# A hybrid decoder layer on one core: another hand-over to attention, and swish made by one ScalarE activation

## The chip, the cores and the metric

The kernel runs on one core of a Trainium2 chip. The metric is the device time of one execution in microseconds; the median of three runs is 1112.57 (1110.75 to 1113.08). TensorE (PE) multiplies, ScalarE (ACT) and VectorE (DVE) work element by element, GpSimd (POOL) too; SP only issues transfers, and ACT and POOL issue some as well. Every engine runs its own list of instructions in order and waits on semaphores for the others.

## What is computed

One decoder layer over 1024 positions of width 1024, all in fp32. Cut to what matters here:

```python
h = rmsnorm(x, ln_pre);  z = h @ w_in
c_val, c_glu, c_gate, q, k, v, a_gate, g_conv, g_attn = split_columns(z)
u  = c_val * sigmoid(c_glu)
c  = silu(layernorm(causal_depthwise_conv31(u) + b_dw, ln_g, ln_b))
ya = ((c @ w_pw) * silu(c_gate)) @ w_br_conv
yb = (sliding_window_sink_attention(rope16(q), rope16(k), v) * silu(a_gate)) @ w_br_attn
x  = x + rmsnorm((sigmoid(g_conv) * ya + sigmoid(g_attn) * yb) @ w_out, ln_post)
x  = x + sigmoid(x @ w_ple_gate) * (p @ w_ple_proj)
```

There are 16 query heads and 2 key heads of 64 values; of each head the first 16 values are rotated by position (rope), the other 48 are not. The window is 128, the block 128.

## The kernel before, in words

Everything lies transposed: 128 partitions hold channels, the 1024 positions run along the free dimension, and a matrix of 1024 channels is 8 rows of 128 x 1024. Every product is made from a high and a low part of its operands: ScalarE rounds a tile to fp32r (`high`, `split_high`, `..._high`), another engine subtracts to get the rest (`tile_low`, `low`, `..._low`), and TensorE adds three products. Nothing is scheduled by a compiler: the order on each engine is written out by hand, and a semaphore names each dependence.

The program's stages on TensorE are: the per-layer embedding product; a few plain tiles of `h @ w_in`; 18 pairs of output rows by a scheme of seven products (`EARLY`, L953), the last of them k and v; two plain tiles Q0 and Q0+1, which are query rows 3 and 7 (L766); attention (`attention(p)`, p from 0 to 15; block n = p // 2 and key head p % 2), in which each p also multiplies one half of a tile of the convolution's gate, C0 + n (L1101); 8 tiles D0 of the attention's gate; 8 tiles E0 for the attention branch; the seven products again, stage F for `c @ w_pw` and stage G for `@ w_br_conv` (`seventh`, L1193), in 4 pairs each; and the two last matrices.

**The turn from the pairs to attention.** Query rows 0, 1, 2, 4, 5 and 6 have been stored to memory (`GATES` rows 3 KT + j) during the pairs; k and v come last, in `ring` (`k_raw`, `v_t`). VectorE rotates several heads in one instruction, so the 16 rotated values of each head are collected: `pack0` holds 16 rows for each of the two key heads and 6 query half rows, `pack1` 6 query half rows. SP issues all of it in this order (L668 to L692): the angle tables `cos_t` and `sin_t`, three rows' `pack` (16-row transfers, two per query row), the two k groups from `k_raw`, the other six `pack`, four `kdup` transfers (the 48 plain values of each key head, to two places), the six whole query rows to `qo`, the weights C0, and then, after the rotation, `unpack(0)` (six 16-row transfers back to `qo`), four to `kdup`, `unpack(1)`, and the weights C0 + 1. `unpack` waits for a finished rotation (`rope_done`) and for all query rows (`q_loaded`, 96).

VectorE (L2192 to L2194) runs `rope(0)` on pack0, `rope(1)` on pack1 and `rope_in_place(0)` on query row 3, four or five full-width steps each, the last two one behind the other through `rope_done` and `last_roped`. The first scores (`scores(0, 0)`, L981) wait for `conv_done`, `k_dup`, `unpacked[0]` and `last_roped`.

**In attention**, for each p ScalarE first reads the gate product of p - 1 (`gate_half`, L1574: a tanh to `tanh_t`, a copy to `gate_val`), splits the next gate weights (`next_high`), copies outputs and turned probabilities, and makes eight exponentials (`exps`, L1549). VectorE finds maxima, makes the gate as (tanh + 1) * value in `ring` (its own `gate_half`, L2254), and normalises. At p = 0 ScalarE's list has `high(C0 // 2, 1)`, the split of the weights C0 + 1, ahead of the first `exps`. The gate is stored to memory and read back in stage F.

**Stage F.** Per pair i, ScalarE copies four products aside (`keep`, L1686), reloads the two gate rows by `load_gates` (L1699), and makes high parts of weights (`block_high`). VectorE's `take` (L2409) combines quarters and multiplies each with its gate half, in `ring`; `block_low` (L2387) makes the low part of the weights that TensorE uses some products later, in the same list. The sums of the results for stage G (`y_sum`, `part_high`, `part_low`) come at the end of pair 3.

The layer norm's swish is a tanh on ScalarE (`norm_tanh`, L1651) and two VectorE steps (`norm_finish`, L2360); the attention's gate a tanh and one VectorE step. The factor 1/2 of x/2 * (1 + tanh(x/2)) is applied later, in the splits.

Of the kernel before, what the change touches and what calls it, by code (L numbers as in the profile page):

```python
# [25 lines left out]
P = 128  # L26
# [9 lines left out]
HD = 64  # L36
# [72 lines left out]
def build(nc, dram):  # L109
    with ExitStack() as ctx:  # L110
# [29 lines left out]
        cos_t = at("cos_t", [S], F32, RE + 12 * KB)  # L140
# [6 lines left out]
        gate_val = at("gate_val", [HALF], F32, RE + 22 * KB)  # L147
# [11 lines left out]
        v_last = at("v_last", [P], F32, GB + 28 * KB - 192)  # L159
# [46 lines left out]
        for name, n in (("half_g", KT), ("half_b", KT), ("two_b", KT), ("mean_sq", 8), ("rstd", 8), ("expo", 8), ("sq_sums", 8), ("sinks", 16),  # L206
                        ("smax", 16), ("nmax", 16), ("esink", 16), ("denom", 16), ("rden", 16)):
            names[name] = at(name, [n], F32, small)
            small += 4 * n
        half_g, half_b, two_b, mean_sq, rstd, expo, sq_sums = (names[n] for n in (  # L210
            "half_g", "half_b", "two_b", "mean_sq", "rstd", "expo", "sq_sums"))
# [31 lines left out]
        tanh_ready = sem("tanh_ready")  # L243
# [30 lines left out]
        gated = sem("gated")  # L274
# [24 lines left out]
        ln_tanh = sem("ln_tanh")  # L299
# [109 lines left out]

        def pack_of(j):  # L410

            return (0, j + 1) if j < 3 else (1, j - 4)
# [175 lines left out]
        def _(sp):  # L588
# [51 lines left out]
            def pack(j):  # L640

                n, c = pack_of(j)
                for par in range(2):
                    sp.dma_start(packs[n][32 * c + 16 * par:32 * c + 16 * par + ROT, :],
                                 GATES[par * HD:par * HD + ROT, 3 * KT + j, :]).then_inc(packed[n], 16)

            def unpack(n):

                sp.wait_ge(rope_done, n + 1)
                sp.wait_ge(q_loaded, 96)  # L650
                for j in range(4 * n, 4 * n + 3):
                    c = pack_of(j)[1]
                    for par in range(2):
                        sp.dma_start(qo[par * HD:par * HD + ROT, j, :],
                                     packs[n][32 * c + 16 * par:32 * c + 16 * par + ROT, :]).then_inc(unpacked[n], 16)
# [4 lines left out]
            sp.dma_start(w_second[:], WALL[:, Q0 + 1 + PLE_STEPS, :]).then_inc(w_loaded[1], 16)  # L660
            sp.wait_ge(spilled[0], 16 * len(SPILLS))
            sp.wait_ge(spilled[1], 16 * len(SPILLS))
            sp.wait_ge(pos_loaded, TRIG_STORED)
            sp.wait_ge(early_made, EARLY_PRODUCTS - 1)
            def rows_of_angles(first, last):
                return TRIG[first:last].rearrange("n (f c) a -> (n f) (c a)", f=8).rearrange("(a r) s -> a r s", a=1)

            for table, first, last in ((cos_t, 0, 1), (sin_t, 1, 3)):  # L668
                count = 8 * (last - first)
                sp.dma_start(table[:], rows_of_angles(first, last).to_broadcast([P // count, count, S])).then_inc(pos_loaded, 16)  # L670
            for j in (0, 1, 2):
                pack(j)
# [3 lines left out]
            for j in (4, 5, 6):  # L676
                pack(j)
            for g in range(2):
                for half in range(2):
                    sp.dma_start(kdup[half * HD + ROT:(half + 1) * HD, g, :],  # L680
                                 k_raw[g * HD + ROT:(g + 1) * HD, :]).then_inc(k_dup, 16)
            for j in (0, 1, 2, 4, 5, 6):
                sp.dma_start(qo[:, j, :], GATES[:, 3 * KT + j, :]).then_inc(q_loaded, 16)
# [4 lines left out]
            for g in range(2):  # L688
                for half in range(2):
                    sp.dma_start(kdup[half * HD:half * HD + ROT, g, :], packs[0][ROT * g:ROT * g + ROT, :]).then_inc(k_dup, 16)  # L690
            unpack(1)
            load_tile(C0 + 1)  # L692
# [62 lines left out]
        def _(pe):  # L755
# [225 lines left out]
            def scores(p, jp):  # L981
# [365 lines left out]
        def _(act):  # L1347
# [175 lines left out]

            act.wait_ge(v_turned, 1)
# [5 lines left out]
            nc.scalar.activation(v_last[lower_half], turned_values[lower_half, NB - 1, :], ACT.Copy).then_inc(v_ready, 1)  # L1530
            query_tile(0)
# [42 lines left out]
            def gate_half(p):  # L1574
# [7 lines left out]
                if p > 1:  # L1582
                    act.wait_ge(gated, p - 1)
                nc.scalar.activation(tanh_t[:, half], gate_bank(p), ACT.Tanh, scale=0.5).then_inc(tanh_ready, 1)
                if p > 0:
                    act.wait_ge(gated, p)
                nc.scalar.activation(gate_val[:], gate_bank(p), ACT.Copy).then_inc((half_free, ps_free[n % 2])[h], 1)

            def spill_gate(n):

                act.wait_ge(gated, 2 * n + 2)
                spill(GATES[:, n + KT, :], n % 2)
# [41 lines left out]
            for m in range(KT):  # L1634
# [6 lines left out]
                split_high(o_hi, m, qo[:, m, :], 0.5)  # L1641
# [9 lines left out]
            def norm_tanh(k):  # L1651

                act.wait_ge(ln_scaled, k + 1)
                if k >= 2:
                    act.wait_ge(ln_full, k - 1)
                nc.scalar.activation((tanh_t, work)[k % 2][:], conv[:, k, :], ACT.Tanh, bias=half_b[:, k:k + 1],
                                     scale=half_g[:, k:k + 1]).then_inc(ln_tanh, 1)

            def c_high(k):
# [5 lines left out]
                nc.scalar.activation(dst, src, ACT.Copy, scale=0.5).then_inc(hi_ready, 1)  # L1665
# [11 lines left out]
            def sum_high(n):  # L1677
# [6 lines left out]
                nc.scalar.activation(s_hi[:, n], sum_of(n), ACT.Copy, scale=0.5).then_inc(s_hi_ready, 1)  # L1684
# [24 lines left out]

            def part_high(name, k):  # L1710
# [9 lines left out]
                nc.scalar.activation(part_split(name, rows)[0], part_raw(name, rows), ACT.Copy, scale=0.5).then_inc(part_hi, 1)  # L1720
# [10 lines left out]
            for m in range(KT):  # L1731
# [6 lines left out]
                for k in norm_beside(m):  # L1738
                    norm_tanh(k)
# [132 lines left out]
        def _(dve):  # L1872
# [131 lines left out]
            own.step(nc.vector.tensor_scalar(half_g[:], cols[:, COL["ln_g"]:COL["ln_g"] + KT], 0.5, None, ALU.mult))  # L2004
            own.step(nc.vector.tensor_scalar(two_b[:], cols[:, COL["b_dw"]:COL["b_dw"] + KT], 2.0, None, ALU.mult))
            own.step(nc.vector.tensor_scalar(half_b[:], cols[:, COL["ln_b"]:COL["ln_b"] + KT], 0.5, None, ALU.mult))
# [185 lines left out]
            rope(0, P, slice(0, S), 128)  # L2192
            rope(1, 96, slice(0, S), 96)
# [60 lines left out]
            def gate_half(p):  # L2254

                n, h = divmod(p, 2)
                half = slice(h * HALF, (h + 1) * HALF)
                dve.wait_ge(tanh_ready, p + 1)
                dve.wait_ge(spilled[n % 2], (n // 2) * 16 + 16 * len(SPILLS))
                if h == 0:  # L2260
# [466 lines left out]
```

## Time and profile before

| | |
|---|---|
| median of three runs | 1112.57 us |
| the profiled execution: its time, its span | 1111.12 us, 1109.3 us |
| granted TensorE clock, mean | 0.995 |
| busy: PE, PEld, DVE, ACT, POOL | 1090.7, 887.9, 884.9, 485.2, 316.2 us |
| DMA | 155.19 MB, mean 140 GB/s |
| chain that ended last: PE | 91% of the span |

The span runs from the first to the last instruction; the execution's time has 1.8 us around it. Times of the views are microseconds from the span's start. "PE busy" counts matmuls in flight. A wait of an engine is idle time, put down to what ended it. A transfer's time to landing runs from its issue until its semaphore has the full count of 16. The granted clock is 1.00 at 2.4 GHz and 0.50 at 1.2 GHz.

### The profile page before, as it was taken

Reading aid. Unit: us, or ns where it says so; the run is one execution under the profiler, and the core shown is the slowest. Engines: PE = TensorE matmul, PEld = TensorE weight load, DVE = VectorE, ACT = ScalarE, POOL = GpSimd, SP = SyncE. Lnnn points to the kernel's source line nnn. Section 1 sums busy time; section 2 is a strip of 40 time slices with the busy share of each in tenths; the row PEclk is TensorE's granted clock in tenths of the full one; section 3 lists DMA queues with packets and bytes.
Section 4 is the critical chain, followed back from the end, with each engine's and each line's share of the span. In section 5 each row is a group of like instructions: output and inputs, shape, how many; then the busy total and the mean of one; then the engine's idle time right before and its main releaser. Section 6 shows DMA issues by size and latency. Waiting matters only on the chain.

```text
span 1109.3 us, 16255 instructions
## 1 busy us (share of the span) xinstructions
PE 1090.7 (98%) x5992; PEld 887.9 (80%) x5992; DVE 884.9 (80%) x1243; ACT 485.2 (44%) x927; POOL 316.2 (29%) x252
## 2 busy tenths in 40 slices
PE   9999999999999998799999999999999999999998
PEld 7888888888888886577777888888888888888887
DVE  5998989999999975598985788777768878466875
ACT  6633343443334432466674442433435426344332
POOL 1068888887888851200000000000000000000000
PEclk9999999999999999899999999999999999999999
DMA  9802231322232329777742111464544843344655
GB/s 343 350 1 78 78 113 42 114 77 77 94 134 77 114 80 236 206 208 198 187 131 77 39 57 38 133 217 143 180 134 129 319 137 127 95 128 138 192 188 189
DMA packets 52976, 155.19 MB, mean 140 GB/s; under 512 B 6281, under 2 KB 7049, under 8 KB 50857
## 3 DMA queue, kind: packets, MB, share of 16 engines
q1 hardware_dynamic: 38216, 96.58, 27.1%
q10 hardware_dynamic: 12384, 40.90, 10.5%
q0 software_dynamic: 2304, 16.78, 6.4%
q8 instruction: 43, 0.70, 0.2%
q14 instruction: 29, 0.23, 0.1%
HBM read 123.86 MB, written 45.19 MB: 152 GB/s over the span
## 4 chain that ended last, share of the span: by engine, by line
PE 91%; DMA 3%; SPq 2%; DVE 2%; ACT 1%; issue 1%; DVEq 0%; ACTq 0%
PE psg L766 31%; PE psg L953 31%; PE psb L1193 11%; PE psg L1101 7%; PE psg L790 2%; PE psg L1072 1%; PE psb L1015 1%; PE psg L1193 1%; DMA qo<-gates 1%; PE psg L873 1%; PE psg L819 1%; PE psg L1146 1%; PE psg L1033 1%; ACT probs L1558 1%; PE psg L1067 1%; DMA p_raw<-pT 1%
## 5 line engine op out<-in xcount | busy, mean ns | idle before, releaser
L1251 POOL TENSOR_TENSOR pair_w<-early_raw,pair_w 128x512 fp32r<-128x512 f32 x117 | 155.5, 1338 | 83.1 <-ACT pair_w L1443 83.1
L953 PE MATMUL psg<-early_hi,pair_w 128*128 128x512 f32 x576 | 177.3, 389 | 0.0
L2095 DVE SCALAR_TENSOR_TENSOR psb<-conv,cols,psb 128x510 f32<-128x510 f32 (+6 forms) x196 | 137.7, 745 | 0.0
L953 PE MATMUL psg<-h_hi,pair_w 128*128 128x512 f32 x432 | 133.0, 389 | 0.0
L953 PEld LDWEIGHTS psg<-early_hi,pair_w 128*128 128x128 f32 x576 | 108.1, 188 | 22.4
L1443 ACT ACTIVATE pair_w<-early_raw 128x512 fp32r<-128x512 f32 x117 | 71.4, 627 | 112.3 <-POOL early_raw L1267 81.1
L1234 POOL TENSOR_TENSOR rstd<-mean_sq,expo 128x4 f32<-128x4 f32 x3 | 3.1, 1020 | 382.9 <-DVE mean_sq L1896 363.4
L953 PE MATMUL psg<-early_lo,pair_w 128*128 128x512 f32 x288 | 112.0, 389 | 0.0
L1882 DVE TENSOR_TENSOR w_lo<-w_raw,w_hi 128x1024 fp32r<-128x1024 f32 x57 | 69.8, 1224 | 41.2 <-ACT w_hi L1356 37.5
L953 PEld LDWEIGHTS psg<-h_hi,pair_w 128*128 128x128 f32 x432 | 81.1, 188 | 16.8
L1356 ACT ACTIVATE w_hi<-w_raw 128x1024 fp32r<-128x1024 f32 x58 | 61.2, 1056 | 65.0 <-PE psg L766 34.6
L2095 DVE SCALAR_TENSOR_TENSOR psb<-fir_sum,fir_taps,psb 128x511 f32<-128x511 f32 (+14 forms) x120 | 89.4, 745 | 0.0
L953 PE MATMUL psg<-h_lo,pair_w 128*128 128x512 f32 x216 | 84.0, 389 | 0.0
L1267 POOL TENSOR_TENSOR early_raw<-early_raw 128x512 f32<-128x512 f32 x54 | 75.0, 1390 | 4.2
L1193 PE MATMUL psb<-s_hi,pair_w 128*128 128x512 f32 x240 | 73.9, 389 | 0.0
L953 PEld LDWEIGHTS psg<-early_lo,pair_w 128*128 128x128 f32 x288 | 54.1, 188 | 11.3
L766 PE MATMUL psg<-h_hi,w_hi 128*128 128x512 f32 x192 | 59.6, 392 | 0.0
L766 PE MATMUL psg<-h_hi,w_lo 128*128 128x512 f32 x192 | 59.2, 389 | 0.0
L766 PE MATMUL psg<-h_lo,w_hi 128*128 128x512 f32 x192 | 59.1, 389 | 0.0
L1675 ACT ACTIVATE pair_w<-block_raw 128x512 fp32r<-128x512 f32 x56 | 34.5, 626 | 41.7 <-PE psb L1193 21.5
L1193 PEld LDWEIGHTS psb<-s_hi,pair_w 128*128 128x128 f32 x240 | 45.0, 188 | 9.4
L1101 PE MATMUL psg<-h_hi,w_hi 128*128 128x512 f32 x128 | 52.1, 407 | 0.0
(348 smaller groups left out, 2511.8 us busy)
## 6 DMA issues: line engine op xcount, KB each, us to landing
w_raw<-weights SPq DMA_DIRECT2D x60, 512.0 KB, 3.6
gates<-ring ACTq DMA_DIRECT2D x30, 512.0 KB, 3.6
w_sums<-w_pairs POOLq DMA_DIRECT2D x12, 1024.0 KB, 8.5
ring<-gates ACTq DMA_DIRECT2D x24, 512.0 KB, 4.4
early_raw<-w_pairs SPq DMA_DIRECT2D x9, 1024.0 KB, 5.5
block_raw<-w_sums SPq DMA_DIRECT2D x32, 256.0 KB, 3.0
early_raw<-w_pairs SPq DMA_DIRECT2D x9, 768.0 KB, 4.6
block_raw<-w_pairs SPq DMA_DIRECT2D x24, 256.0 KB, 3.7
```

Of the source, the lines that this page charges most:

```text
L766: mm = nc.tensor.matmul(psg[:, slot, h * HALF:(h + 1) * HALF], w[:, wslot, (wk + k) * P:(wk + k + 1) * P], r[:, k, h * HALF:(h + 1) * HALF ...
L790: mm = nc.tensor.matmul(psg[:, slot, h * HALF:(h + 1) * HALF], w[:, slot, k * P:(k + 1) * P], r[:, k, h * HALF:(h + 1) * HALF], start=(k = ...
L953: mm = nc.tensor.matmul(bank, pair_w[:, at_w, w, k * P:(k + 1) * P], r[:, k, :], start=(not onto and k == 0 and m == 0), stop=(k == KP - 1 ...
L1101: mm = nc.tensor.matmul(gate_bank(p), w[:, t % 2, k * P:(k + 1) * P], r[:, k, half], start=(k == 0 and m == 0), stop=(k == KT - 1 and m == 2))
L1193: mm = nc.tensor.matmul(bank, pair_w[:, at_w, w, k * P:(k + 1) * P], r[:, k, :], start=(not onto and k == 0 and m == 0), stop=(k == KP - 1 ...
L1251: nc.gpsimd.tensor_tensor(pair_w[:, at_w, 1, :], early_source(s, n), pair_w[:, at_w, 0, :].bitcast(F32), ALU.subtract).then_inc(early_spli ...
L1267: nc.gpsimd.tensor_tensor(early_block(s, out), early_block(s, a), early_block(s, b), ALU.add).then_inc(early_summed, 1)
L1356: nc.scalar.activation(w_hi[:, j % 2, :], w_raw[:, j % 2, :], ACT.Copy).then_inc(w_hi_ready, 1)
L1443: nc.scalar.activation(pair_w[:, early_slot(b), 0, :], early_source(s, n), ACT.Copy).then_inc(early_split_hi, 1)
L1675: nc.scalar.activation(pair_w[:, pair_slot(b), 0, :], block_raw[:, b % 7, :], ACT.Copy).then_inc(pair_hi, 1)
L1882: nc.vector.tensor_tensor(w_lo[:, slot, :], w_raw[:, slot, :], w_hi[:, slot, :].bitcast(F32), ALU.subtract).then_inc(w_lo_ready, 1)
L2095: own.step(stt(acc[:, shift:], source[:, 0:HALF - shift], weight, acc[:, shift:], ALU.mult, ALU.add))
```

## The change

- The rotary values are loaded one transfer per query row (`rotary_rows`: 32 rows, both heads' 16 rows of that query row), all six ahead of the k rows. Only the plain 48 rows of each head go to `qo` from memory (`plain_rows`: four transfers of 48 x 3 rows), and `unpack` no longer waits for them; the first scores do.
- `cos_t` is loaded earlier, in its own place; the weights C0 are loaded right behind the k rows, C0 + 1 ahead of `unpack`.
- The `kdup` transfers go out on ScalarE's queue: four right after the last k quarter, four at `rope_done` 1.
- Swish is one ScalarE activation (`Silu`): for the attention's gate, for the layer norm with its scale and bias, and for the convolution's gate in stage F, once it is back in `ring` (`swish_gates`, ahead of which the raw product was stored). VectorE's steps for them go, and the factors 1/2 in the splits.

```diff
+            def rotary_rows(n):
+                for j in range(3):
+                    rows = GATES.rearrange("(par h) j s -> j par h s", par=2)[3 * KT + 4 * n + j, :, 0:ROT, :]
+                    first = 32 * (1 - n) + 32 * j
+                    sp.dma_start(packs[n][first:first + 32, :], rows).then_inc(packed[n], 16)
+            def plain_rows(n, par):
+                rows = slice(par * HD + ROT, par * HD + HD)
+                sp.dma_start(qo[rows, 4 * n:4 * n + 3, :], GATES[rows, 3 * KT + 4 * n:3 * KT + 4 * n + 3, :]).then_inc(q_loaded, 16)
...
             sp.wait_ge(pos_loaded, TRIG_STORED)
+            load_table(cos_t, 0, 1)
...
+            load_table(sin_t, 1, 3)
+            rotary_rows(0)
+            rotary_rows(1)
             main_read(sp, len(EARLY) - 1)
             for g in range(2):
                 sp.dma_start(packs[0][ROT * g:ROT * g + ROT, :], k_raw[g * HD:g * HD + ROT, :]).then_inc(packed[0], 16)
...
             load_tile(C0)
+            for n in range(2):
+                for par in range(2):
+                    plain_rows(n, par)
+            load_tile(C0 + 1)
             sp.wait_ge(conv_done, KT)
             sp.dma_start(mixed[:], CONST[:, 1, :]).then_inc(masks_loaded, 16)
             unpack(0)
...
             unpack(1)
-            load_tile(C0 + 1)
...
+                    pe.wait_ge(q_loaded, 64)
...
+            act.wait_ge(rope_done, 1)
+            for g in range(2):
+                for half in range(2):
+                    act.dma_start(kdup[half * HD:half * HD + ROT, g, :], packs[0][ROT * g:ROT * g + ROT, :]).then_inc(k_dup, 16)
...
-                nc.scalar.activation(tanh_t[:, half], gate_bank(p), ACT.Tanh, scale=0.5).then_inc(tanh_ready, 1)
-                if p > 0:
-                    act.wait_ge(gated, p)
-                nc.scalar.activation(gate_val[:], gate_bank(p), ACT.Copy).then_inc((half_free, ps_free[n % 2])[h], 1)
+                nc.scalar.activation(ring[:, n % 2, half], gate_bank(p), ACT.Copy).then_inc((half_free, ps_free[n % 2])[h], 1)
...
-                nc.scalar.activation(tanh_t[:], psg[:, j, :], ACT.Tanh, scale=0.5).then_inc(tanh_ready, 1)
+                nc.scalar.activation(tanh_t[:], psg[:, j, :], ACT.Silu).then_inc(ps_free[j], 1)
...
+                nc.scalar.activation(conv[:, k, :], conv[:, k, :], ACT.Silu, bias=col("ln_b", k), scale=col("ln_g", k)).then_inc(ln_full, 1)
...
+            def swish_gates(i):
+                for j in range(2):
+                    act.wait_ge(gate_loaded[j], (i + 5) * 16)
+                    nc.scalar.activation(ring[:, j, :], ring[:, j, :], ACT.Silu).then_inc(gates_ready, 1)
...
             keep(F, 0, P6)
+            swish_gates(0)
             block_high(6)
...
+                    if g == F and i > 0 and n == P6:
+                        swish_gates(i)
...
-            rope(0, P, slice(0, S), 128)
-            rope(1, 96, slice(0, S), 96)
+            rope(0, P, slice(0, S), 80)
+            rope(1, 96, slice(0, S), 48)
...
+                if g == F:
+                    dve.wait_ge(gates_ready, 2 * i + row + 1)
```

How the table loads and the old 16-row groups differ in form from the new ones is in the order of SP's transfers (destination and source, and the size of the destination). SP at the turn, before:

```order
L670 DMA cos_t<-trig 128x1x1024
L670 DMA sin_t<-trig 128x1x1024
L644 DMA pack_70<-gates 16x1024 x6
L675 DMA pack_70<-ring 16x1024 x2
L644 DMA pack_71<-gates 16x1024 x6
L680 DMA kdup<-ring 48x1024 x4
L683 DMA qo<-gates 128x1024 x6
L592 DMA w_raw<-weights 128x1024
L686 DMA mixed<-masks 128x128
L654 DMA qo<-pack_70 16x1024 x6
L690 DMA kdup<-pack_70 16x1024 x4
L654 DMA qo<-pack_71 16x1024 x6
```

and changed:

```order
L657 DMA cos_t<-trig 128x1x1024
L657 DMA sin_t<-trig 128x1x1024
L638 DMA pack_70<-gates 32x1x1024 x3
L638 DMA pack_71<-gates 32x1x1024 x3
L673 DMA pack_70<-ring 16x1024 x2
L585 DMA w_raw<-weights 128x1024
L643 DMA qo<-gates 48x3072 x4
L585 DMA w_raw<-weights 128x1024
L680 DMA mixed<-masks 128x128
L651 DMA qo<-pack_70 16x1024 x6
L651 DMA qo<-pack_71 16x1024 x6
```

The k rows now stand behind all six rotary transfers, kdup has left the queue, and the second weight tile stands ahead of `unpack`. In both, the source of `cos_t` is 16 copies of 8 rows and that of `sin_t` 8 copies of 16 rows, outermost dimension first; the source of a new rotary transfer is 2 groups (`par`) of 16 rows.

ScalarE at the start of stage F (`kept` and `kept_q` are products set aside, `pair_w` the high parts of weights), before:

```order
L1675 ACTIVATE pair_w<-block_raw 128x512 x2
L1697 ACTIVATE kept<-psb 128x512
L1675 ACTIVATE pair_w<-block_raw 128x512
L1697 ACTIVATE kept_q_119<-psb 128x512
L1675 ACTIVATE pair_w<-block_raw 128x512
```

and changed:

```order
L1672 ACTIVATE pair_w<-block_raw 128x512 x2
L1694 ACTIVATE kept<-psb 128x512
L1711 ACTIVATE ring<-ring 128x1024 x2
L1672 ACTIVATE pair_w<-block_raw 128x512
L1694 ACTIVATE kept_q_118<-psb 128x512
L1672 ACTIVATE pair_w<-block_raw 128x512
```

The two full-width swishes stand behind `keep` of the third product (P6), in each of the four pairs.

## Rows read from the trace of the kernel before

**Rows 1.** Waits of PE over the whole span: us in total, times, longest.

```profile
PE psb L1015 <- DMA kdup<-pack: 10.0, 1, 10.0
PE psg L1033 <- DVE probs L2239: 2.3, 1, 2.3
...
PE psg L1072 <- ACT gate_val L1587: 0.6, 2, 0.3
```

**Rows 2.** Busy time by stretch around the turn: stretch, its length, engines, PEclk, DMA share, GB/s.

```profile
439.30:442.60 3.30, 0.00 (x1) 0.00 (x0) 3.23 (x4) 0.24 (x1) 0.00 (x0) 0.98 0.65 228
442.60:449.20 6.60, 0.00 (x0) 0.00 (x0) 1.99 (x2) 1.73 (x2) 4.07 (x2) 0.50 0.72 114
449.20:452.80 3.60, 3.53 (x20) 3.04 (x21) 2.12 (x4) 0.00 (x0) 0.00 (x0) 0.51 0.93 336
452.80:458.00 5.20, 5.20 (x28) 4.05 (x28) 3.79 (x16) 0.74 (x1) 0.88 (x1) 1.00 0.99 270
```

**Rows 3.** Timeline of SP at the turn: start, us taken, the transfers issued.

```profile
414.67 0.70 SPq L670 DMA_DIRECT2D sin_t<-trig  x1
...
418.18 1.25 SPq L675 DMA_DIRECT2D pack<-ring  x2
419.47 3.51 SPq L644 DMA_DIRECT2D pack<-gates  x6
...
441.17 3.68 SPq L654 DMA_DIRECT2D qo<-pack  x6
...
451.22 17.57 SPq L592 DMA_DIRECT2D w_raw<-weights  x3
```

**Rows 4.** Timeline of DVE: first and last step of the three rotations.

```profile
428.17 1.32 DVE L2167 STREAM_SHUFFLE rtmp<-pack 128x1024 f32<-128x1024 f32 x1
...
443.41 1.22 DVE L2189 TENSOR_TENSOR qo<-work,rtmp 16x1024 f32<-16x1024 f32 x1
```

**Rows 5.** Issues at 419.4, 420.3, 422.9, 425.0 (KB, us to landing); packets from 434 to 438.

```profile
pack<-ring SPq DMA_DIRECT2D x1, 64.0 KB, 9.2
pack<-gates SPq DMA_DIRECT2D x1, 64.0 KB, 4.2
...
pack<-gates SPq DMA_DIRECT2D x2, 64.0 KB, 4.7
...
kdup<-ring SPq DMA_DIRECT2D x1, 192.0 KB, 5.1
pack<-gates SPq DMA_DIRECT2D x1, 64.0 KB, 8.0
...
kdup<-ring SPq DMA_DIRECT2D x1, 192.0 KB, 8.6
...
DMA packets 448, 1.63 MB, mean 409 GB/s; under 512 B 49, under 2 KB 49, under 8 KB 448
```

**Rows 6.** ACT before the first exponentials (timeline); groups of ACT: busy, mean ns.

```profile
457.26 1.06 ACT L1356 ACTIVATE w_hi<-w_raw 128x1024 fp32r<-128x1024 f32 x1 [12.93 <-DMA w_raw<-weights]
...
L1632 ACT ACTIVATE ring<-conv 128x1024 f32<-128x1024 f32 x8 | 8.5, 1064 | 0.3
```

**Rows 7.** Timelines of ACT, DVE and PE in stage F, pair 0.

```profile
784.77 0.60 ACT L1697 ACTIVATE kept<-psb 128x512 f32<-128x512 f32 x1 [2.83 <-PE psb L1193]
...
783.28 0.69 DVE L2437 TENSOR_TENSOR y_raw<-quarter,ring 128x512 f32<-128x512 f32 x1
...
787.29 0.62 PE L1193 MATMUL psb<-s_hi,pair_w 128*128 128x512 f32 x2
```

**Rows 8.** Timelines of ACT, DVE and PE from pair 3 of F to stage G.

```profile
841.89 0.60 ACT L1697 ACTIVATE kept<-psb 128x512 f32<-128x512 f32 x1 [0.61 <-PE psb L1193]
...
841.88 0.69 DVE L2437 TENSOR_TENSOR y_raw<-quarter,ring 128x512 f32<-128x512 f32 x1
...
857.68 0.73 PE L1193 MATMUL psb<-c_hi,pair_w 128*128 128x512 f32 x2 [0.19 <-DVE c_lo L2469]
```

More of the change, by code:

```diff
@@ L638, in load_tile, with load_table @@
                 load_weights(t + PLE_STEPS, t % 2, t + 1)
[L640 to L645, printed above, removed]
+            def rotary_rows(n):
[6 more added lines that the diff above has]
+                sp.dma_start(qo[rows, 4 * n:4 * n + 3, :], GATES[rows, 3 * KT + 4 * n:3 * KT + 4 * n + 3, :]).then_inc(q_loaded, 16)
             def unpack(n):
                 sp.wait_ge(rope_done, n + 1)
-                sp.wait_ge(q_loaded, 96)
-                for j in range(4 * n, 4 * n + 3):
-                    c = pack_of(j)[1]
+                for j in range(3):
                     for par in range(2):
-                        sp.dma_start(qo[par * HD:par * HD + ROT, j, :],
-                                     packs[n][32 * c + 16 * par:32 * c + 16 * par + ROT, :]).then_inc(unpacked[n], 16)
+                        first = 32 * (1 - n) + 32 * j + ROT * par
+                        sp.dma_start(qo[par * HD:par * HD + ROT, 4 * n + j, :], packs[n][first:first + ROT, :]).then_inc(unpacked[n], 16)
+            def load_table(table, first, last):
+                count = 8 * (last - first)
+                rows = TRIG[first:last].rearrange("n (f c) a -> (n f) (c a)", f=8).rearrange("(a r) s -> a r s", a=1)
+                sp.dma_start(table[:], rows.to_broadcast([P // count, count, S])).then_inc(pos_loaded, 16)
             sp.wait_ge(early_made, EARLY_LAST)
@@ L660, in _ @@
             sp.dma_start(w_second[:], WALL[:, Q0 + 1 + PLE_STEPS, :]).then_inc(w_loaded[1], 16)
+            sp.wait_ge(pos_loaded, TRIG_STORED)
+            load_table(cos_t, 0, 1)
             sp.wait_ge(spilled[0], 16 * len(SPILLS))
             sp.wait_ge(spilled[1], 16 * len(SPILLS))
-            sp.wait_ge(pos_loaded, TRIG_STORED)
             sp.wait_ge(early_made, EARLY_PRODUCTS - 1)
[L665 to L672, printed above, removed]
+            load_table(sin_t, 1, 3)
+            rotary_rows(0)
+            rotary_rows(1)
             main_read(sp, len(EARLY) - 1)
@@ L1530, in _ @@
             nc.scalar.activation(v_last[lower_half], turned_values[lower_half, NB - 1, :], ACT.Copy).then_inc(v_ready, 1)
+            act.wait_ge(rope_done, 1)
+            for g in range(2):
+                for half in range(2):
+                    act.dma_start(kdup[half * HD:half * HD + ROT, g, :], packs[0][ROT * g:ROT * g + ROT, :]).then_inc(k_dup, 16)
             query_tile(0)
@@ L1649, in load_gate, with norm_swish @@
                 act.dma_start(ring[:, slot, :], GATES[:, r, :]).then_inc(gate_loaded[slot], 16)
-            def norm_tanh(k):
+            def norm_swish(k):
                 act.wait_ge(ln_scaled, k + 1)
[L1654 to L1657, printed above, removed]
+                nc.scalar.activation(conv[:, k, :], conv[:, k, :], ACT.Silu, bias=col("ln_b", k), scale=col("ln_g", k)).then_inc(ln_full, 1)
             def c_high(k):
@@ L2358, in norm_scale @@
                 nc.vector.tensor_tensor(conv[:, k, :], conv[:, k, :], sums[:], ALU.mult).then_inc(ln_scaled, 1)
-            def norm_finish(k):
-                dve.wait_ge(ln_tanh, k + 1)
-                own.step(nc.vector.tensor_scalar(conv[:, k, :], conv[:, k, :], col("ln_g", k), col("ln_b", k), ALU.mult, ALU.add))
-                own.wait()
-                stt(conv[:, k, :], (tanh_t, work)[k % 2][:], 1.0, conv[:, k, :], ALU.add, ALU.mult).then_inc(ln_full, 1)
             def c_low(k):
@@ L2371, in c_low @@
                                     (slice(1, 3), k - KP, conv[:, k, :].rearrange("p (h s) -> p h s", h=2)))
-                stt(c_lo[:, blocks, row, :], src, 0.5, c_hi[:, blocks, row, :].bitcast(F32),
-                    ALU.mult, ALU.subtract).then_inc(lo_ready, 1)
+                nc.vector.tensor_tensor(c_lo[:, blocks, row, :], src, c_hi[:, blocks, row, :].bitcast(F32),
+                                        ALU.subtract).then_inc(lo_ready, 1)
             def gate(a2, j, r):
@@ L2485, in _ @@
                 if m == 5:
-                    norm_finish(KT - 1)
                     c_low(KT - 2)
```

82 lines of the change are left out of this document (27 added, 55 removed).

## The prediction

> **What bounds the kernel now.** I began with the busy shares of the page's first part (the table above): TensorE is busy for 1090.7 of 1109.3 us, so the change can win only part of 18.6 us, the clock's losses apart, while any new wait of TensorE is paid in full. Then what TensorE waits for [rows 1]: 10.0 us are one wait, the first scores on kdup, 2.3 us one other, the first turn of probabilities, and two further attention waits make 0.6 us; most of the rest is the program's start and end. By stretches [rows 2], TensorE does nothing from 439.3 to 449.2; its granted clock falls to half 3.3 us after it stopped (0.98, then 0.50 and 0.51) and is back at full 3.6 us after it resumed (1.00). So about 1.8 us of work time is lost too (3.6 us at half speed).
>
> What ends that wait is the issuing of SP [rows 3]. unpack(0) waits for all q rows, its six transfers go out from 441.17, then the four of kdup, one every 0.6 us, and the last lands 2.4 us after issue, at 449.2. VectorE has been ready since 444.6 [rows 4]: three rotations run one behind the other, from 428.14, when the k rows have landed in pack0, to 443.41 + 1.22. That is 16.5 us from landing to last_roped, and nothing in the change shortens it.
>
> **The turn: what is better.** kdup's last rows go out on ScalarE's queue at rope_done 1, 5 us after the rotations start, and unpack(0) no longer waits for q. Both are then done before the third rotation; the 4.6 us from 444.6 to 449.2 are gone. What remains is: scores start 16.5 us after the k rows land. Call that landing X (428.1 before).
>
> **The turn: when X is.** SP's queue does not land in order. The two k rows are issued from 418.18 on, the second at 418.8, and it lands 9.2 us later, at 428.0; a row group of pack1 issued after them, at 419.5, lands 4.2 us after issue, at 423.7, and of the six for pack1 the first three land early (by 425), the last late, 8.0 us after issue [rows 3, 5]. A landing is a full count over 16 engines and a group of 16 rows gives each one row; so half of the engines ran ahead and half were behind. Both tables have 128 rows, but cos_t is written as 16 copies of 8 rows, sin_t as 8 copies of 16: if a transfer is dealt out by its outermost dimension, sin_t is on 8 engines with 16 rows each, and just these 8 are behind. The new rotary_rows has "par" outermost, with two values: by the same reading each of its six transfers puts 16 rows on each of **two** engines, 96 rows on each in all, and the k rows stand behind them in the same queue, where each engine has its share.
>
> The Trainium skill (DMA: Bandwidth & Descriptors, "Why a DMA increments its semaphore by 16 and not by 1") says this as a rule: a copy from SP or ACT uses the largest number of engines up to 16 that divides the slowest dimension of both sides. By it 2 engines for rotary_rows, 8 for sin_t; the landings of [rows 5] agree.
>
> Price of a row of 4 KB: in 434 to 438, wide transfers on all engines, 1.63 MB in 4 us over 16 engines is 25.5 GB/s each, 0.16 us a row [rows 5]. Dear end: the engines behind have 24 table rows and 8 small ones between 415.3 and 428.0, 0.40 us a row. Now X:
> - sin_t, 16 rows per engine: 2.6 us (0.16) to 6.4 (0.40). I take 0.36, as it was the slow one: from 415.3 to 421.
> - 96 rows: 15.4 us at 0.16; at 0.25, half way up, 24. I take 15.4, since only two engines move: 436.4.
> - the four kdup transfers, now on ScalarE's queue from 418, share these engines, 12 rows each. Floor 1.9 us; before, they landed about 1.8 us apart (issued 0.65 us apart, 5.1 and 8.6 us to landing), 0.6 us a row, 7.2. I take 4; and 1 for two k rows.
>
> X = 441.5, between 435.5 (0.16 everywhere) and 447. Scores start at X + 16.5 = **458.0** where they started at 449.3: +8.7 us (bounds +2.7 and +14.2). Behind the k rows the same two engines have C0, the plain rows and C0+1, 8 + 36 + 8 rows, 8.3 us at 0.16: to 450, and unpack(0) and kdup by 452, all before 458. If a row costs 0.3 there they come at 458 too. POOL's weight sums start some 7 us later than before and have until 765, so nothing. The clock is at half when TensorE resumes, as before; 3.6 us of half speed before, up to 6 now, so 0 to +1.5, I take +0.3.
>
> **Behind the turn.** ScalarE's first exponentials were held in order behind the split of tile C0+1, whose load SP issued only at 451.22: w_hi at 457.26, and the exponentials right after it, at 458.2 [rows 3, 6], though VectorE had the maxima ready at 454. That load now goes ahead of unpack and has landed by 450. Relative to the scores, the exponentials start 4 us earlier, normalised probabilities are ready about 10 us after the scores start, and TensorE asks for them some 11.5 us after (a row of scores and 5.7 us of gate products, part of it at half speed, the second scores, a third of the second gate products): the 2.3 us go, and the 0.6 with them, as the ScalarE and VectorE chain gets 4 us ahead. **-2.9** (at worst 0).
>
> **Attention, tile D0, layer norm.** Out go, on VectorE, 16 gate steps, 8 of the attention gate and 16 of the layer norm, on ScalarE 16 copies, and one table load of ScalarE comes in. TensorE waits for none of the removed steps except as counted above [rows 1], so 0; the cover is TensorE's own work, a tile of 48 matmuls at a time. If that cover were thin the table load would show once, by a microsecond or two.
>
> **The first matmul stage of the seven-product scheme (F).** Here the change adds two ScalarE steps of 1.06 us per pair (128x1024, price of ring<-conv [rows 6]) and a wait: VectorE's take needs the swish, and ScalarE makes it only after keep(P6). What is queued behind take on VectorE is block_low. Two places:
> - pair 0: take wrote y_raw at 783.28, then came the low parts of blocks 4 and 5. Now keep(P6) at 784.77, swish 785.26 to 786.3, y_raw to 787.05, block 4 to 787.7; TensorE begins that product at 787.29 [rows 7]. **+0.4**.
> - pair 3: keep(P6) 841.89, swish to 843.45; y_raw stood at 841.88. From there VectorE has no pause until 855.1, and TensorE already waits 0.19 at 857.68 for c_lo, its end [rows 8]. 1.57 us later there is 1.57 later here: **+1.6**.
> In pairs 1 and 2 VectorE pauses between its steps, and a block's low part is made five products ahead of its use: 0. Sum +2.0; floor 0.5 if the chain has slack I don't see, ceiling 3.
>
> **Sum.** +8.7 + 0.3 - 2.9 + 2.0 = +8.1 on 1111.12, the profiled execution's own time: 1119.2. That execution is 1.45 us below the median of the runs, 1112.57; I go between: **1119.5**.
>
> **Rivals.**
> - The rotary rows spread over all engines like the old 16-row groups. For: half as many issues, and nothing in the trace has an outermost 2. Against: the landings above. Then on the engines behind: sin_t to 421, 12 + 2 rows at 0.4, kdup 2 to 4: X about 429, scores at 445.5, -3.8; but the clock fell at 442.6 and stayed down until 452.8, so half speed costs 3.6 instead of 1.8 us. -3.8 + 1.8 - 2.9 + 2.0 = -2.9: **1108**. This is the case on the other side; it decides once X is before 435, where the same sum is 0.
> - The two engines are slower than 0.16 us a row, or unpack(0) and the plain rows behind them end last instead of the rotations: X 447 or landing at 464, **1125**.
> - The turn as forecast but F's chain has more slack: **1117**, inside my range.
> - The table switch or ScalarE's order starves D0: one load, against tiles of 48 matmuls: 1121, 2 in 100.
>
> **How the numbers follow.** The two-engine case has 0.84 with its slower half (1119.5; 0.6, and the slow one 0.24), the all-engines case 0.13, the rest 0.03. Floor of the two-engine case: +2.7 - 2.9 + 0.5 gives 1111.4 to 1112.9 by either base; its bulk lies above 1113. The range 1112 to 1126 leaves out the faster case and the far end of the slow one. About 0.2% (2.2 us) is what a measurement of this kernel can tell from no change: faster 0.13, within 0.08 (low end of the two-engine case), slower 0.79.
>
> **What would show it.** Right: TensorE's wait at the first scores near 19 us, and named after VectorE's last rotation; VectorE's first rotation waiting until about 441 with few GB/s on the DMA engines from 422 on; no wait at the first turn; a new 1.6 us wait at 857 (plus the shift) on c_lo. Wrong: a DMA share near 1 and X before 430 in that stretch, or last_roped long done while TensorE waits for qo rows.

## The result, and the profile after

The changed kernel takes **1128.32 us** (median of 4 runs, 1127.78 to 1128.66), the kernel before in the same comparison 1112.82: a ratio of 1.0141 (95% interval 1.0123 to 1.0158), 15.5 us slower. Forecast were 1119.5, with a range of 1112 to 1126. The side was right, the size was not: it lies above the range.

The span of the profiled execution is 1126.0 us (1109.3 before), the mean granted clock 0.986 (0.995). TensorE is busy for 1091.2 us, as before, so the 16.7 us are waits and the clock. What TensorE waits for, over the whole span, without the waits at the start; these rows answer to [rows 1]:

```profile
PE psb L1006 <- DVE qo L2193: 27.4, 1, 27.4
PE psb L1184 <- DVE c_lo L2452: 1.4, 1, 1.4
...
PE psb L1184 <- DVE pair_w L2371: 0.3, 1, 0.3
```

The first scores wait 27.4 us instead of 10.0, and what ends the wait is VectorE's last rotation, no longer a transfer. The waits of 2.3 and 0.6 us in attention are gone. The next two rows are stage F's. SP's list at the turn, against [rows 3] (start, time taken, transfers):

```profile
413.68 0.70 SPq L657 DMA_DIRECT2D sin_t<-trig  x1
414.44 3.88 SPq L638 DMA_DIRECT2D pack<-gates  x6
418.37 7.40 SPq L673 DMA_DIRECT2D pack<-ring  x2
...
426.44 2.41 SPq L643 DMA_DIRECT2D qo<-gates  x4
...
454.06 8.83 SPq L651 DMA_DIRECT2D qo<-pack  x12
```

VectorE, first step of the rotations and last (start, length, in brackets the idle time before and what ended it), against [rows 4]:

```profile
449.06 0.01 DVE L2171 LOAD_MASK_SELECT rtmp<-pack  x1 [34.76 <-DMA pack<-ring]
...
464.91 1.22 DVE L2193 TENSOR_TENSOR qo<-work,rtmp 16x1024 f32<-16x1024 f32 x1
```

The k rows landed at 449.0; the forecast had X = 441.5, before it was 428.1. From there the rotations take 17.1 us to 466.13 (forecast 16.5), and the scores start at 466.4. By stretches (stretch, its length, busy time of PE, PEld, DVE, ACT and POOL, PEclk, DMA share, GB/s), against [rows 2]:

```profile
439.00:443.00 4.00, 0.00 (x0) 0.00 (x0) 0.00 (x0) 0.00 (x0) 0.00 (x0) 0.76 0.90 157
...
430.00:438.00 8.00, 8.00 (x37) 6.63 (x36) 0.00 (x0) 0.00 (x0) 0.00 (x0) 1.00 1.04 172
446.00:454.00 8.00, 0.00 (x0) 0.00 (x0) 4.86 (x5) 0.00 (x0) 0.00 (x0) 0.50 0.13 50
...
466.40:471.00 4.60, 4.60 (x22) 3.89 (x23) 3.11 (x7) 0.00 (x0) 0.88 (x1) 0.50 0.78 191
...
471.50:472.00 0.50, 0.50 (x3) 0.42 (x2) 0.47 (x3) 0.50 (x4) 0.00 (x0) 0.68 1.02 213
```

Three things are to be seen. From 446 to 454 the DMA share is 0.13, two engines of 16 (0.125), and they move 50 GB/s: 25 each, 0.16 us per 4 KB. These are the last rows of the packs and, from 449 on, what stands behind them on the same two engines. That is the forecast's mechanism and its price. But from 430 to 438 the share is 1.04: all engines are busy, at only 172 GB/s, or 0.40 us per 4 KB (16 x 8 us x 1.04 over 1.37 MB). The loads behind the k rows run then, beside the two engines' rows, and they are slow. Third, the clock fell 2 us after TensorE had stopped (0.76 over the four us from 439) and is back within the half microsecond from 471.5, so TensorE works 5.4 us at half speed instead of 3.6: 0.9 us more. The sum against before: +17.4 (wait) + 0.9 (clock) - 2.9 (attention's waits) + 1.5 (F) = +16.9, where the spans differ by 16.7.

### The profile page after: what moved, and what is told of

Its sections match the earlier page's. It is cut to its first block, busy times and chain, and to the rows that moved or that the text cites. A ratio compares the mean times of both kernels' runs of the same rounds, so it can differ in the third digit from the quotient of the medians.

```text
span 1126.0 us, 16186 instructions
## 1 busy us (share of the span) xinstructions
PE 1091.2 (97%) x5992; PEld 888.0 (79%) x5992; DVE 850.1 (76%) x1201; ACT 484.8 (43%) x920; POOL 316.6 (28%) x252
## 4 chain that ended last, share of the span: by engine, by line
PE 92%; DVE 3%; DMA 3%; SPq 1%; issue 0%; ACT 0%; DVEq 0%; ACTq 0%
PE psg L756 31%; PE psg L943 30%; PE psb L1184 11%; PE psg L1092 8%; DMA pack<-ring 2%; PE psg L780 2%; PE psb L1006 2%; PE psg L1063 1%; PE psg L1184 1%; PE psg L863 1%; PE psg L809 1%; PE psg L1137 1%; PE psg L1024 1%; PE psg L1058 1%; DMA p_raw<-pT 1%; PE psb L863 1%
## 5 line engine op out<-in xcount | busy, mean ns | idle before, releaser
L1242 POOL TENSOR_TENSOR pair_w<-early_raw,pair_w 128x512 fp32r<-128x512 f32 x117 | 160.5, 1381 | 82.1 <-ACT pair_w L1434 81.9
L1258 POOL TENSOR_TENSOR early_raw<-early_raw 128x512 f32<-128x512 f32 x54 | 71.2, 1318 | 4.2
```

Source lines behind the costliest of these rows:

```text
L1242: nc.gpsimd.tensor_tensor(pair_w[:, at_w, 1, :], early_source(s, n), pair_w[:, at_w, 0, :].bitcast(F32), ALU.subtract).then_inc(early_spli ...
L1258: nc.gpsimd.tensor_tensor(early_block(s, out), early_block(s, a), early_block(s, b), ALU.add).then_inc(early_summed, 1)
```

## The experiments

Theory A was that two engines hold the k rows back; rivals were the place in the queue (B) and kdup's transfers on ScalarE's queue (C). All ratios are against the kernel before, run in the same comparison; its median lies between 1111.30 and 1112.08 there. Two edited kernels that were not compared with each other are compared by their distances from it.

**16-row groups again.** One thing of the change undone:

```diff
-                    rows = GATES.rearrange("(par h) j s -> j par h s", par=2)[3 * KT + 4 * n + j, :, 0:ROT, :]
-                    first = 32 * (1 - n) + 32 * j
-                    sp.dma_start(packs[n][first:first + 32, :], rows).then_inc(packed[n], 16)
+                    for par in range(2):
+                        first = 32 * (1 - n) + 32 * j + ROT * par
+                        sp.dma_start(packs[n][first:first + ROT, :],
+                                     GATES[par * HD:par * HD + ROT, 3 * KT + 4 * n + j, :]).then_inc(packed[n], 16)
...
```

> The change with one thing undone: the rotary rows go as twelve transfers of 16 rows instead of six of two groups of 16; they stay ahead of the k rows. Theory A (each transfer of two groups lies on two DMA engines, and the k rows stand behind them there): the k rows land at about 428 instead of 449, VectorE's first rotation starts then, scores 16.5 to 17 us later at 445, PE's wait 27.4 becomes 5 to 6 us; with the F stage still dearer by 1.5 and the exponentials' 3 us gained the time is about 1108.5 (1106 to 1111). Theory B (what delays the k rows is that twice as many rotary rows stand ahead of them in SP's queue, whatever their shape): first rotation not before 438, wait over 15, 1117 or more. Theory C (the kdup transfers from ScalarE's queue take the engines' time): hardly better than the change, 1125 or more.

Measured: 1117.49, ratio 1.0053 (1.0035 to 1.0071). VectorE began at 433.39. Of the 20.9 us by which the change's k rows come later than before (449.06 against 428.14), 15.7 are gone with the form of the transfers: theory A. The other 5.2 stay, and 4.8 of them are issuing (the k rows went out at 422.97, before at 418.18): this part is the place in the queue, which A had at nothing, since it expected a landing at 428. B as the whole cause is out (first rotation not before 438); that its time and its wait, 1117 or more and over 15, came true is no support for it, since another transfer ended the wait. A's wait of 5 to 6 us and its 1108.5 were missed: a second wait stands where the first was. TensorE's waits, and SP's list (start, time taken, transfers):

```profile
PE psb L1007 <- DMA qo<-pack: 15.7, 1, 15.7
```

```profile
424.89 2.07 SPq L644 DMA_DIRECT2D qo<-gates  x4
...
438.46 8.85 SPq L652 DMA_DIRECT2D qo<-pack  x12
```

unpack(0), issued from 438.46 on, landed near 454.8. The rotations had ended at 450.5. So all-engines rows alone do not rescue the change.

**pack1 behind the k rows**, in the change (one call, `rotary_rows(1)`, moved; three transfers).

> The change with the three transfers of pack1 behind the k rows. Theory A: 48 rows fewer ahead of the k rows on the two engines, so the first rotation starts about half way between 421 and 449, at 435, but the second one, for pack1, starts where it did, about 449 (all 96 rows are through then); scores 11 to 12 us after that, 461, time 1122 to 1125. The difference of the two landings over 48 is the price of a row on an engine: 0.25 to 0.32 us, where the prediction took 0.16. Theory B: both rotations early, 1113 or less. Theory C: both late, first rotation over 440.

Measured: 1129.49, ratio 1.0156 (1.0133 to 1.018): no gain at all, where A expected 1122 to 1125. First rotation at 438.56, second at 455.15: 16.6 us for 48 rows on each engine, 0.35 us a row. The two landings came in the order that A has, but 3.6 and 6 us later than it said, at a price above its 0.25 to 0.32.

**The two-group transfers alone, in the kernel before.**

> The kernel before with one thing of the change: the rotary rows in transfers of two groups. Theory A: slower than before, by about 10 us: first rotation at 435 to 438, second held until all 96 rows are through, 445 to 450, scores at about 460 (449 before), time 1120 to 1126. Theory B: order as before, so no slower, first rotation by 428, 1112 or 1113. Theory C: the same as B, since kdup's transfers stand where they stood.

Measured: 1124.51, ratio 1.0118 (1.0096 to 1.014). As A said: this edit alone costs 12.9 us. That is not all from the k rows, which come only 5.8 us later than before (433.92). pack1's rotation waits until 445.52, the rotations end at 456.8, and the first scores start at 466.3 (A said about 460), when the rotated k values have landed in kdup: the whole q loads and `unpack(0)` run late as well. VectorE, the starts of the first two rotations:

```profile
433.92 0.01 DVE L2166 LOAD_MASK_SELECT rtmp<-pack  x1 [18.52 <-DMA pack<-ring]
...
445.52 0.01 DVE L2166 LOAD_MASK_SELECT rtmp<-pack  x1 [6.57 <-DMA pack<-gates]
```

Here wide q loads stood behind, and 48 rows took 11.6 us: 0.24 us a row.

**kdup's plain rows behind the first rotation**, in the change.

> The change with the four transfers of kdup's plain rows issued behind the first rotation. Theory A: they have 12 rows on each of the two engines; at 0.25 to 0.35 us a row the first rotation comes 3 to 4 us earlier, 445, and the time is about 1125. Theory C: first rotation before 435, time about 1112. Theory B: 1 or 2 us at most.

Measured: 1131.75, ratio 1.0193 (1.0166 to 1.0219). From sin_t's issue to the first rotation it is 33.7 us instead of 35.4: kdup's share was 1.7 us, where A expected 3 to 4; this number is the one of theory B, 1 or 2. The time is worse at least in part because eight transfers now stand in ScalarE's list ahead of the copy of query row 3, for which VectorE's third rotation waits (461.46, 4.2 us). C, first rotation before 435, is out.

**What makes a row dear.** Rotary rows at 0.16 us with the engines to themselves, 0.24 to 0.35 otherwise. Theory N: the other engines write at the same time, and slowly, because a transfer to 16 or 48 partitions does not reach full rate. Theory L: it is the number of rows. Four runs.

> The change with the plain q rows (four transfers to 48 partitions, 36 rows of 4 KB per engine) replaced by the six full-height transfers of before (128 partitions, 48 rows per engine); unpack waits for them, as before. Theory N (the two engines' rows are slow because the other engines write at the same time to few partitions; transfers over 128 partitions run at 0.16 us a row and leave room): the first rotation starts 3 to 8 us earlier than the change's 449, at 441 to 446, though a third more rows stand behind the k rows; time 1121 to 1126. Theory L (what counts is the number of rows in the queue, or the two engines have one price of 0.28 us by themselves): first rotation at 449 or later, time 1128 or more.

Edit: `plain_rows` replaced by six loads `qo[:, j, :] <- GATES[:, 3 * KT + j, :]`, as before. Measured: 1126.37, ratio 1.0137 (1.012 to 1.0154). First rotation at 447.33 with sin_t issued at 415.28: 32.1 us after it, against 35.4. Faster by 3.3 though more rows stand behind: N rather than L, at the low end of what it expected by that clock, and missed by 1 us as an absolute time. The wait of the first scores is 25.4 us and is ended by `unpack(0)`, no longer by the rotations.

> The change with everything behind the k rows in SP's queue (C0, the plain rows, C0+1) held back until both packs have landed, so that the two engines work nearly alone. Theory N: they then move a row in about 0.16 us, the prediction's price, and the first rotation starts at 438 to 442 where the change has 449; the held loads then land in time for the scores or a little behind them; time 1120 to 1125. Theory L: a row costs the two engines 0.28 us alone as well, first rotation at 447 or later, time 1130 or more.

Edit: two waits, `packed[0]` and `packed[1]`, ahead of `load_tile(C0)`. Measured: 1128.26, ratio 1.0149 (1.0132 to 1.0165). The first rotation starts at **440.11**. By stretches, the packs' landing and then the plain rows:

```profile
430.00:439.00 9.00, 9.00 (x42) 7.40 (x40) 0.00 (x0) 0.00 (x0) 0.00 (x0) 1.00 0.13 53
443.00:457.00 14.00, 0.00 (x0) 0.00 (x0) 13.47 (x13) 2.88 (x3) 3.24 (x2) 0.50 1.05 168
```

Alone, the two engines have a share of 0.13 and move 53 GB/s, 0.155 us per 4 KB. From sin_t's issue it is 26.0 us. So 9.3 of the change's 35.4 us come from the loads behind the k rows being under way at the same time. Full-height loads at that time, the run before this one, still cost 6.0 of them; N's "leave room" holds for a third of the effect. The forecast's 441.5 fits this kernel, as a sum; its terms were not measured one by one, and kdup's was too dear. Nothing is gained in time, where N expected 1120 to 1125 and the held loads in time for the scores or a little behind, since the held loads then take theirs: with all engines busy they move at 168 GB/s, and unpack(0), behind them, ended TensorE's wait at 467.05.

> As the run that holds the loads back until the packs have landed, but the plain q rows go by tile (twelve transfers of 48 rows of 4 KB instead of four with rows of 12 KB). If it is the few partitions that make these rows slow (0.42 us per 4 KB with all engines at it), the stretch in which they move keeps its 150 to 170 GB/s and the first scores start at 465 to 468 as there. If it is the 12 KB rows, it rises over 300 GB/s and the scores start 7 us earlier, about 459.

Edit: the same, with `plain_rows` as twelve transfers of one query row each. Measured: one run, 1125.89.

```profile
443.00:457.00 14.00, 0.00 (x0) 0.00 (x0) 13.15 (x13) 2.88 (x3) 3.48 (x2) 0.50 1.05 175
```

The first scores start at 464.99. The 12 KB rows are not the cause: 175 GB/s with 4 KB rows.

> The change with both undone: 16-row groups and full-height q loads (the order of the queue, C0+1 ahead of unpack, kdup on ScalarE's queue and the swish stay). With 16-row groups alone the first scores waited 15.7 us for unpack(0), issued at 438.5 and landed at 454.8. Theory N (the plain q rows to 48 partitions hold the queue at 150 to 250 GB/s and unpack stands behind them): the full-height loads move at 300 GB/s or more, unpack(0) lands by 450, the wait is 8 to 11 us and the time 1111 to 1114, faster than with 16-row groups alone though 12 rows more per engine are loaded. If what unpack waits for is only the number of rows ahead of it, the wait stays at 15 us or more and the time at 1117 or above.

Edit: 16-row groups and full-height q loads together, all else as changed, but for unpack's wait for the q rows, which comes back with them. Measured: **1111.84**, ratio 0.9998 (0.9988 to 1.0007): the whole loss is gone. The stretch in the run with 16-row groups alone, the same stretch here, and TensorE's wait here:

```profile
430.00:438.00 8.00, 8.00 (x37) 6.62 (x36) 4.52 (x5) 0.00 (x0) 0.00 (x0) 1.00 1.03 185
```

```profile
430.00:438.00 8.00, 8.00 (x37) 6.64 (x36) 5.24 (x7) 0.00 (x0) 0.00 (x0) 1.00 1.00 349
```

```profile
PE psb L1007 <- DVE qo L2194: 10.5, 1, 10.5
```

349 GB/s instead of 185 at the same full share, and unpack is hidden again behind the rotations. So the form of the plain q rows is the second part of the loss: 5.7 us between these two kernels (5.9 above before, and 0.2), with a third more rows loaded. With the two-group transfers in place the same edit is worth next to nothing in time (15.1 us above before, the change 15.5): there the rotations still end late, at 464.4. The Trainium skill (SBUF — State Buffer, "Door 1: The DMA port swizzle") says that a transfer's bandwidth goes by how many of 16 ports its partitions reach, that partitions 0 to 63 reach only half of them, and 16 partitions a quarter. The plain rows of either head half lie within one such half. The traces agree in size, about half the rate (168 to 185 in three runs with the plain rows, against 349); that ports are the mechanism, rather than something else of narrow transfers, no run here isolates.

**The swish alone, with the turn of before.**

> The change's swish (attention, tile D0, layer norm, stage F) with the turn of before: 16-row groups, order of SP's queue and kdup's transfers as before. The turn costs what it cost before, 10 us of wait at the first scores and about 2 at the first probabilities; stage F costs 1.5 us more (1.4 us of PE's wait on c_lo where 0.2 stood, 0.3 at pair 0). Expected 1.5 us above before, 1113 to 1114; if the swish also cost something in attention or at D0, 1116 or more, with a new wait in PE's list.

Measured: 1113.48, ratio 1.0020 (1.0010 to 1.0029), so 2.2 us (1.1 to 3.2).

```profile
PE psb L1014 <- DMA kdup<-pack: 10.9, 1, 10.9
PE psb L1192 <- DVE c_lo L2451: 1.4, 1, 1.4
...
PE psg L1032 <- DVE probs L2242: 1.1, 1, 1.1
PE psb L1014 <- ACT probs L1557: 0.5, 1, 0.5
PE psb L1192 <- DVE pair_w L2370: 0.3, 1, 0.3
```

Nothing new in attention, at D0 or in the layer norm; F's two waits are those of the change. ScalarE's one table load more (1.28 us) shows in no wait.

**The swish of F, row by row.**

```diff
+            swish_gates(0, (0,))
             keep(F, 0, P6)
-            swish_gates(0)
+            swish_gates(0, (1,))
...
+                    if g == F and i > 0 and n == P6:
+                        swish_gates(i, (0,))
                     if n in (P1, P6, Q5, P7) and AT[g, i, n] > Q5:
                         keep(g, i, n)
...
-                    if g == F and i > 0 and n == P6:
-                        swish_gates(i)
+                    if g == F and i > 0 and n == Q5:
+                        swish_gates(i, (1,))
```

> The swish with the turn of before, and in stage F the swish of the first gate row goes ahead of keep(P6), that of the second row behind keep(P6) at pair 0 and behind keep(Q5) at the others. If the F term is what the prediction says (VectorE's product waits for two swishes that stand behind keep(P6)), the waits of 1.4 us on c_lo and 0.3 on pair_w shrink to 0.5 or less together, and the time is 1 to 1.5 us under the run with the swish alone, equal to before within 0.1 per cent. If the price of F lies elsewhere, no difference.

Measured: 1111.88, ratio 0.9996 (0.9988 to 1.0005). The wait on pair_w is gone, that on c_lo is 0.6, just over the 0.5 expected; its one place:

```profile
858.35 0.74 PE L1192 MATMUL psb<-c_hi,pair_w 128*128 128x512 f32 x2 [0.62 <-DVE c_lo L2454]
```

So F's price was in that order, as the prediction placed it.

**Two better turns.** The first reorders more:

> A turn built on what the runs showed: 16-row groups, cos_t early as in the change, C0 and q rows of the first group (full height) ahead of unpack(0), those of the second behind it, kdup's plain rows on ScalarE's queue after the v copies, and VectorE rotates pack0, then q tile 0, and pack1 last, since the first scores do not need pack1. Expected: first rotation by 430, scores about 11 to 12 us after it, 440 to 442, hardly behind PE's end of the pair stage (439); waits of 2 to 4 us at the second scores or first probabilities; the clock's fall goes. 1100 to 1105. If the loads behind the k rows end last instead (the first scores named after qo or kdup by DMA), 1106 to 1110.

Measured: 1115.75, ratio 1.0044 (1.0027 to 1.0061), a miss on both of its expectations. The first rotation came at 426.38, but the q rows that unpack(0) waits for landed only at 439.8, and unpack(1) stood behind the second three: TensorE waits twice on qo<-pack, 12.5 us together.

> The swish with the turn of before, and three small moves in it: cos_t is loaded early (as in the change), kdup's rotary rows and half of unpack(0) go out on ScalarE's queue, which is idle there, and C0+1 goes ahead of unpack(1). The wide q loads stay ahead of unpack(0). Expected against the run with the swish alone: first rotation 2 us earlier, the q rows landed at about 440, unpack(0) through by 444 to 445 and kdup long before, so the wait at the first scores 5 to 7 us where it was 10.9; the waits at the first probabilities (1.1 and 0.5) go. 1106 to 1109, faster than before. If ScalarE's issues share the engines' slow time instead, the wait stays over 9 us and the time at 1112.

Two places of it, as against the change:

```diff
+            sp.wait_ge(q_loaded, 96)
+            unpack(0, (0,))
+            load_tile(C0 + 1)
+            unpack(1)
...
+            act.wait_ge(q_loaded, 96)
+            for j in range(3):
+                act.dma_start(qo[HD:HD + ROT, j, :], packs[0][32 * (j + 1) + ROT:32 * (j + 1) + 2 * ROT, :]).then_inc(unpacked[0], 16)
```

Measured: 1108.16, ratio 0.9965 (0.9954 to 0.9977), as expected: the wait is 7.0, and attention's are gone. What each of the moves is worth by itself no run tells.

> Both at once: the moves in the turn and the split swish. The two are 350 us apart and should add: 1105 to 1108, the fastest of all.

Measured: **1106.95**, ratio 0.9954 (0.9941 to 0.9966). The fastest kernel of the study, 5 us under before. What is left at the turn and in F:

```profile
PE psb L1011 <- DMA qo<-pack: 6.2, 1, 6.2
...
PE psb L1189 <- DVE c_lo L2458: 0.6, 1, 0.6
```

## Why the prediction was wrong in size

By its own steps:

- **Which engines** (two for the new transfers): right. A share of 0.13 with 50 and 53 GB/s shows it, and the edit alone in the old kernel costs 12.9 us.
- **The price of a row on them. This is the step that failed**: "96 rows: 15.4 us at 0.16; at 0.25, half way up, 24. I take 15.4, since only two engines move". Not only two moved. The prediction's own sign for being right was "few GB/s on the DMA engines from 422 on"; from 430 to 438 all of them were busy. From sin_t's issue (in the fifth line cos_t's, which went with it) to the first rotation, with the rows that each of the two engines had to take until then:

| kernel | rows | us | us a row |
|---|---|---|---|
| the change | 126 | 35.4 | 0.28 |
| kdup's plain rows late | 114 | 33.7 | 0.30 |
| full-height q loads | 126 | 32.1 | 0.25 |
| pack1 behind the k rows | 78 | 24.3 | 0.31 |
| two-group transfers in the kernel before | 74 | 19.1 | 0.26 |
| the rest held back | 126 | 26.0 | 0.21 |

  At 0.25 us in the prediction's own sum the 96 rows take 24 us and X is 450; measured are 449.0. Its dear bound, 447, did not carry that price either: with 6.4 us for sin_t, 7.2 for kdup and 1 for the k rows it leaves 17.1 us for the 96 rows, 0.18 us a row. The rows of before had shown both prices, [rows 5] the cheap one in the stretch of wide transfers, and the "dear end" of 0.40 in the stretch of narrow ones. The prediction chose by what the two engines would do, and not by what stood behind them in the queue: 576 rows x 4 KB to 48 partitions each. Holding these, C0 and C0 + 1 back measures what they cost the k rows, 9.3 us.
- **The rows behind the k rows**: the same low price was taken for these, 8.3 us and `unpack(0)` landed by 452. Where X was as forecast, in the run that holds them back, `unpack(0)` ended TensorE's wait at 467.05 and the time was 1128.26. So a right X would not have saved the forecast for that order; both groups of rows were priced too low.
- **kdup's share**: 4 us taken, 1.7 measured. **Rotations**: 16.5 against 17.1.
- **The clock**: +0.3 taken of 0 to 1.5, measured 0.9: half speed lasts 5.4 us and not 3.6.
- **Behind the turn**: -2.9, right in number: both waits are gone, and the first exponentials follow the scores by 4.7 us (466.38 to 471.08) where it was 9.0. The edited kernels with C0 + 1 ahead of unpack(1) have neither wait either, the run with the swish alone keeps 1.6 us of such waits. But a late start of the scores does the same: the two-group transfers in the kernel before, with C0 + 1 still behind unpack(1) and no swish, have neither wait and the same 4.7 us, and so has the run with the swish split. Whether the moved load or the late scores took them away in the change is not shown.
- **Stage F**: +2.0 taken, 1.5 by the waits, both places named. 2.2 (1.1 to 3.2) by the runs. The split swish takes it back, but for 0.4 us of the wait on c_lo.
- **Attention, D0, layer norm**: 0, right; no row of TensorE's waits names them.
- **The rivals.** The slow case (1125, 0.24) was the true one, but the price of 0.25 was never carried into the range's top: 96 rows at 0.25 put X at 450 and the time at 1128. The all-engines rival was priced at 1108; its kernel takes 1117.5, since it ignored both the dozen issues ahead of the k rows and unpack(0) behind slow plain rows. Its landing, 433.4, lies before the 435 at which the prediction saw the turn to the faster side, and it was slower than before by 5.9 us.

## What to carry to other kernels

Read a queue's engines before its bytes: the transfers here whose outermost dimension is 2 ran on two engines, and what stood behind them in that queue waited there. Loading fewer bytes to fewer partitions can be slower than loading the whole tile: here 576 rows to 48 partitions lost 5.7 us against 768 rows to 128. Loads of the same queue that run at the same time on the other engines are part of the price: they made 9.3 of 35.4 us here. When two prices for the same operation stand in a trace, take the one of the stretch that looks like the new program, not the one of the cleanest stretch.

## What the runs showed of the hardware

- **Issuing itself took longer behind the two-engine transfers.** The two transfers pack<-ring took SP 7.40 us to issue in the change (7.07 and 6.61 in two variants, 4.11 with kdup's plain rows late), 1.25 with 16-row groups. That alone moves the loads behind from about 419.6 to 425.8. The likely reason is that the two engines' part of the queue is full; no run shows it.
- **A VectorE step with two inputs waited for GpSimd.** In the first of the two reordered turns one step of a rotation took 3.35 us, its neighbours 1.22; it began just after GpSimd's w_lo and ended 1.1 us after it:

```profile
435.12 2.40 POOL L1240 TENSOR_TENSOR w_lo<-w_raw,w_hi 128x1024 fp32r<-128x1024 f32 x1 [11.81 <-ACT w_hi L1352]
```

```profile
435.24 3.35 DVE L2198 TENSOR_TENSOR qo<-work,rtmp 16x1024 f32<-16x1024 f32 x1
438.62 1.22 DVE L2199 TENSOR_TENSOR qo<-work,rtmp 16x1024 f32<-16x1024 f32 x1
```

  In the change the same meeting makes 1.80 of 1.23 us at 460.69, which is the 0.6 us by which its rotations ran over the forecast. In the kernel before it was the other way round: VectorE's last step of the rotations began first (443.41) and took its 1.22 us, and w_lo, begun at 443.50, took 3.32 where it is 2.40 above. The Trainium skill (SBUF — State Buffer, "SBUF: two separate sides") calls it an exclusive lock that is held for a whole instruction; the traces agree with that.
